# Moving the query product of the HGRN decay levels to GpSimd and one convolution tap back to VectorE, with the exponents of each level computed in its own turn

## The reference

```python
proj = xn @ w_in + b_in
(h_q, h_f_fwd, h_f_bwd, h_i, h_g, m_q, m_k, m_v, m_o, gates...) = split_cols(proj, IN_SPLITS)
q_h = to_heads(silu(h_q));  v_h = to_heads(h_i)
lf  = lower_bounded_log_forget(h_f, lb);  k = -expm1(lf)          # for each direction
# HGRN2: S_t = diag(f_t) S_{t-1} + k_t v_t^T,  o_t = S_t^T q_t,  both directions added
#   score(t, s) = sum_d q[t,d] * k[s,d] * exp(cum[t,d] - cum[s,d])
hgrn_out = head_rmsnorm(o_h) * silu(h_g)
qk  = silu(centred_dwconv(concat(m_q, m_k), conv_w, conv_b))      # 5 taps along the tokens
# mLSTM over qk, m_v and the gates, both directions, then the output projection
```

## Time and profile before

| | us |
|---|---|
| median of 3 runs | 1890.41 |
| the runs | 1887.72, 1890.41 and one of 5112.27 |
| the profiled execution, its own time | 1887.72 |
| its span on the core | 1885.9 |
| TensorE busy | 1780.3 |
| VectorE busy | 964.3 |
| ScalarE busy | 665.6 |
| GpSimd busy | 155.8 |

### The profile page before, as it was taken

One profiled execution on the slowest core, in us unless ns is written; L12 is line 12 of the kernel. 1 busy time (PEld: TensorE's weight loads), 2 busy tenths in 40 slices (PEclk: granted clock), 3 DMA queues, 4 the chain that ended last, 5 costly groups with the idle time before them and its releaser, 6 DMA issues.

```text
span 1885.9 us, 18182 instructions
## 1 busy us (share of the span) xinstructions
PE 1780.3 (94%) x6946; PEld 1246.3 (66%) x6946; DVE 964.3 (51%) x1328; ACT 665.6 (35%) x993; POOL 155.8 (8%) x160
## 2 busy tenths in 40 slices
PE   7999898988899999998999898989998999999997
PEld 1378643355688888886765455446886778888886
DVE  5657555355464424433476676377543254434343
ACT  2531244312343313325442542543543243323132
POOL 0302200014200000003000000023200100000001
PEclk9999999999999999999999999999999999999999
DMA  9324310421213232223131111101521122222331
GB/s 320 113 92 157 112 35 11 152 94 45 91 51 117 79 112 90 89 84 117 45 111 64 70 45 45 48 0 63 184 89 46 45 89 90 89 89 89 113 109 44
DMA packets 98353, 166.26 MB, mean 88 GB/s; under 512 B 3371, under 2 KB 39723, under 8 KB 98092
## 3 DMA queue, kind: packets, MB, share of 16 engines
q1 hardware_dynamic: 94524, 152.63, 23.5%
q0 software_dynamic: 3760, 12.72, 2.1%
HBM read 163.23 MB, written 2.10 MB: 88 GB/s over the span
## 4 chain that ended last, share of the span: by engine, by line
PE 84%; DVE 6%; ACT 5%; issue 2%; DMA 1%; POOL 1%; SPq 0%; DVEq 0%; ACTq 0%; POOLq 0%
PE bank L726 12%; PE bank L727 12%; PE bank L728 12%; PE bank L759 6%; PE bank L760 6%; PE bank L764 5%; PE bank L713 4%; PE bank L939 3%; PE bank L780 3%; PE bank L1107 3%; PE bank L1165 2%; PE bank L969 2%; PE bank L829 1%; PE bank L982 1%; PE bank L909 1%
## 5 line engine op out<-in xcount | busy, mean ns | idle before, releaser
L2650 POOL TENSOR_TENSOR arena<-arena 128x512 f32<-128x512 f32 (+1 forms) x56 | 72.7, 1308 | 985.4 <-ACT arena L1335 981.6
L759 PE MATMUL bank<-xn_hi,weights_hi 128*128 128x512 f32 x320 | 127.4, 398 | 6.2 <-ACT xn_hi L1320 6.2
L760 PE MATMUL bank<-xn_hi,weight_slots_lo 128*128 128x512 f32 x320 | 127.1, 397 | 0.0
L1315 ACT ACTIVATE weights_hi<-weight_slots 128x2048 fp32r<-128x2048 f32 (+2 forms) x46 | 77.0, 1725 | 121.5 <-DMA weight_slots<-in_ffn_w_down 67.1
L1871 ACT ACTIVATE weights_hi<-weight_slots 128x2048 fp32r<-128x2048 f32 x30 | 55.8, 1908 | 162.8 <-DMA weight_slots<-in_w_up 109.1
L713 PE MATMUL bank<-arena,weight_slots 128*128 128x512 f32 x256 | 112.2, 592 | 0.0
L726 PE MATMUL bank<-xn_hi,weights_hi 128*128 128x512 f32 x288 | 112.0, 389 | 0.0
L727 PE MATMUL bank<-xn_lo,weights_hi 128*128 128x512 f32 x288 | 112.0, 389 | 0.0
L728 PE MATMUL bank<-xn_hi,weight_slots_lo 128*128 128x512 f32 x288 | 112.0, 389 | 0.0
L2607 DVE TENSOR_TENSOR weight_slots_lo<-weight_slots,weights_hi 128x2048 fp32r<-128x2048 f32 x30 | 67.4, 2289 | 86.3 <-ACT weights_hi L1871 86.3
L1302 ACT ACTIVATE arena<-bank 128x512 f32<-128x512 f32 (+3 forms) x110 | 54.7, 538 | 139.6 <-PE bank L728 50.6
(11 more groups left out here) (402 smaller groups left out, 3822.8 us busy)
## 6 DMA issues: line engine op xcount, KB each, us to landing
weight_slots<-in_w_in SPq DMA_DIRECT2D x30, 1024.0 KB, 7.2
weight_slots<-in_ffn_w_up SPq DMA_DIRECT2D x22, 1024.0 KB, 7.2
weight_slots<-in_w_mod SPq DMA_DIRECT2D x16, 1024.0 KB, 7.6
weight_slots<-in_w_up SPq DMA_DIRECT2D x16, 1024.0 KB, 6.4
weight_slots<-in_w_down SPq DMA_DIRECT2D x16, 1024.0 KB, 6.4
arena<-in_w_mod POOLq DMA_DIRECT2D x32, 256.0 KB, 3.4
weight_slots<-in_w_out SPq DMA_DIRECT2D x8, 1024.0 KB, 7.4
weight_slots<-in_w_xkv SPq DMA_DIRECT2D x8, 1024.0 KB, 7.5
```

The costliest lines, as they stand in the source:

```text
L759: mm(ps[:, 0:width], wh(k, m), x2[0][:, k, 0:width], start=k == 0, stop=False)
L760: mm(ps[:, 0:width], wl(k, m), x2[0][:, k, 0:width], start=False, stop=False)
L1315: A(high(kind, n)[:, a:b], W[:, s_, a:b], ACT.Copy).then_inc(w_hi, 1)
L2650: G.tensor_tensor(acc, acc, sq[i % 2][:, 0:width], ALU.add).then_inc(sq_added, 1)
```

## The change

There are three edits, which belong together.

1. The product of B with the queries (18 instructions of 128x1024) goes from VectorE to GpSimd. GpSimd's list gets it between the load of the bias rows and the wait for ho_3; a step of level 0, which has no such product, gets a one-element copy that only raises B_ready. TensorE waits for B_ready at every step, level 0 included.
2. The centre tap of the convolution and the semaphore conv_mid go: VectorE computes it as its own first instruction of five, and ScalarE only evicts the product.
3. VectorE's order in a step: the exponents of step n now stand in step n, ahead of the masked copies of the step before and of `keys_decayed` of n, and no longer one step ahead.

```diff
@@ TensorE, level()
                 pe.wait_ge(sem("A_ready"), n + 1)
-                if lev:
-                    pe.wait_ge(sem("B_ready"), n - hp)
+                pe.wait_ge(sem("B_ready"), n + 1)
@@ ScalarE, projection_out()
                     free(A(raw_[:, m, :], ps[:], ACT.Identity, bias=b), f"{kind}_{m}")
-                if kind in ("mq", "mk"):
-
-                    o, c0 = (mq, 0) if kind == "mq" else (mk, HC)
-                    evicted(act, f"{kind}_{m}")
-                    if kind == "mk":
-                        act.wait_ge(sem("conv_done"), HC)
-                    A(o[:, m, :], raw_[:, m, :], ACT.Identity, scale=pc("mlstm_conv_w_2", 16 + c0 + m),
-                      bias=pc("mlstm_conv_b_2", c0 + m)).then_inc(sem("conv_mid"), 1)
@@ VectorE, keys_decayed()
                 V.tensor_tensor(Ar, Ar, split(kb, hp, lev)[1], ALU.mult).then_inc(sem("A_ready"), 1)
-                dve.wait_ge(sem("decay_B"), n - hp)
-                B_ = AB[n % 2][1]
-                V.tensor_tensor(B_, B_, q2[:, 1024 * hp:1024 * hp + 1024], ALU.mult).then_inc(sem("B_ready"), 1)
@@ VectorE, projection_out()
-                    dve.wait_ge(sem("conv_mid"), c0 + m + 1)
+                    link(V.tensor_scalar(o[:, m, :], r_[:, m, :], w[2], pc("mlstm_conv_b_2", c0 + m), ALU.mult, ALU.add))
@@ VectorE, the loop
                         for hp, lev in groups[g]:
-                            i = steps.index((hp, lev))
-                            if i == 0:
-                                exponents(hp, lev)
+                            exponents(hp, lev)
+                            scores_out()
                             keys_decayed(hp, lev)
-                            scores_out()
-                            if i + 1 < len(steps):
-                                exponents(*steps[i + 1])
                             pending.append((hp, lev))
@@ GpSimd, after the load of the bias rows
+            for m in range(HC):
+                evicted(pool, f"hq_{m}")
+            for hp, lev in steps:
+                n = steps.index((hp, lev))
+                q_ = q2[:, 1024 * hp:1024 * hp + 1024]
+                B_ = AB[n % 2][1]
+                if lev == 0:
+                    G.tensor_copy(pool_note[:], eps[:]).then_inc(sem("B_ready"), 1)
+                else:
+                    pool.wait_ge(sem("decay_B"), n - hp)
+                    G.tensor_tensor(B_, B_, q_, ALU.mult).then_inc(sem("B_ready"), 1)
```

More of the change, by code:

```diff
@@ L2714, in _ @@
             load(tiles(82, 2), io["bias_rows"].partition_broadcast(P).rearrange("p (a t) -> p a t", a=2), "bias_rows")
+            steps = hgrn_steps()
+            for m in range(HC):
[9 more added lines that the diff above has]
+                    G.tensor_tensor(B_, B_, q_, ALU.mult).then_inc(sem("B_ready"), 1)
             done(pool, "ho_3")
```

## The result

The changed kernel took 1903.81 us, the median of five runs (1901.11 to 1907.23), against 1887.72 before, the median of five too: two more executions of the kernel before have come to the three in the table above. The ratio is 1.0078, 95% interval 1.0056 to 1.01, or 14.7 us more (10.6 to 19). It is taken over more executions than the medians, eleven of the changed kernel from 1895.12 to 1907.23 us, so it isn't quite the ratio of the two medians, which differ by 16.1 us. The forecast was 1903.0, with 13.4 us more by its sum and 1 more for the clock. The profiled execution took 1901.32.

What follows compares the result with a forecast made beforehand. TensorE, busy for 94% of the span, was the bound, with VectorE's rounds slightly longer (8.98 against 8.66 us) in the mq and mk part. Terms summed to +13.4 us, 1901.1; allowing for the median and 1 us of clock, 1903, range 1892 to 1912.

Steps and rivals of the forecast that it cites:

- GpSimd's product, 2.37 us: Query product of 128x1024 on GpSimd: 2.37 us, from a line between lengths 512 and 2048; bounds 1.29 and 4.52.
- Both engines at once: GpSimd's product and VectorE instructions with two SBUF operands run one after the other, costing VectorE 2.17 us per product.
- Which instruction is blocked: On VectorE, the second half of the keys or an exponent takes 2.7 to 2.9 us instead of 0.68 in most rounds.
- After mq_0: VectorE's eviction, centre tap, taps and the level's chain make the level ready at 1051.6 against 1048.64: +2.9 us.
- After mq_1: VectorE's round is 10.47 us against TensorE's 8.66: +1.8 us.
- Level 512: First pair, level 512 behind level 256: 6.0 us where it was 5.04, a term of +1.0 us.
- Clock: Longer waits of TensorE can also cost clock: 1 us added to the sum.
- Norms: Norms of heads 0 and 1: ScalarE's silu starts after mq_3's eviction without the 0.81 us tap, -0.9 us.
- Behind mk_3: TensorE already waited 2.39 us there for ScalarE's table; VectorE is now late by about as much: -0.2 us.
- No blocking: Rival, 13%: GpSimd's product runs beside VectorE in the stage, so the terms sum to 4.7 us: 1894 us.
- Not slower: Rival, 5%: VectorE's round shrinks from 8.98 to 8.3 us, waits at level 512 and behind mk_3 go: -5, 1883.
- The clock falls as well: Rival, 15%: TensorE's longer waits bring the half clock, three falls of 1.2 to 3.5 us each: +7, 1910 us.

Runs made afterwards that it cites:

- spare kernels: Two kernels: the kernel before, with GpSimd also computing a 128x1024 product nobody needs (ratio 1.0075), or filling tiles with zeros instead (ratio 1.0001).
- the spare writes: The kernel before, with GpSimd also filling two free tiles twice with zeros that nobody needs: 1890.00 against 1890.32 us, ratio 1.0001.
- one level each: The kernel before with each of the 20 decay levels behind a TensorE product of its own, none sharing one: 1872.39 against 1890.32 us, ratio 0.9913.

## Why the prediction was right, point by point

- *GpSimd's product, 2.37 us.* It takes 2.34 undisturbed. The mean of 3.05 in the page is over my 2.4 to 2.8, since the records count the time in which GpSimd stands ready and lets VectorE pass. I had named 3 us and more as a sign of being wrong that would put the mv levels over 8.66; it came, and the mv levels stayed 8.7 us apart.
- *Both engines at once*, the term that decides: right. 2.83 us for 0.68 is 2.15 of blocking where I had 2.17, a key half or an exponent is held like this in 11 of the 18 rounds, and the pair of spare kernels shows it by itself. The product alone cost 8.3 us.
- *Which instruction is blocked*: half right. I named a key half or an exponent. In the rounds behind mq_0 and mk_1 it was the next centre tap, which I had priced by its length alone, and in that behind mk_2 in part (1.01 us). There GpSimd let both key halves pass, so that the level waited for its product and not, as I had it, for the second half behind it. The sum is nearly the same: from the first exponent at 1045.01 to level 128 at 1052.23 are 7.2 us, as forecast.
- *After mq_0*: forecast +2.9, measured 3.7 - 0.6 = +3.1. *After mq_1*: forecast +1.8, measured +4.2, in the second profile +1.7. The step that failed in the first is "by then GpSimd stands ready, its product goes first": it stood ready at 1059.13 and let six instructions go ahead. It cost nothing in the end, because those six included the exponents of level 512.
- *Level 512*: in sum 6.25 forecast, 6.5 and 6.4 measured.
- *Clock.* I gave it 1 us. The slices of the kernel after (length, busy PE, PEld, DVE, ACT, POOL, then the granted clock):

```profile
1060.00:1070.00 10.00, 6.01 (x23) 4.84 (x22) 8.33 (x7) 2.77 (x4) 8.37 (x3) 0.72 0.01 2
1070.00:1080.00 10.00, 10.00 (x30) 5.89 (x29) 3.55 (x5) 3.41 (x7) 0.00 (x0) 0.94 0.00 0
1170.00:1180.00 10.00, 8.41 (x32) 4.55 (x31) 10.00 (x11) 2.80 (x3) 5.39 (x2) 1.00 0.13 49
```

  Behind the wait of 3.99 us TensorE ran at 1.2 GHz for a while, so level 512 took 4.86 us instead of the 3.69 in the earlier trace rows: +1.2. At the last level 512 it was the other way round, 5.38 against 6.10: -0.7. The slice from 1170, at 0.68 before, is at 1.00 now, because VectorE and with it the wait came later. In sum +0.5 here, and some 3 in the second profile: the 1 lies between, with more spread than I gave it. Nor does a wait's length settle it: I had noted that the 3.10 us at 1062 cost no clock, and with the spare writes the same wait did, 1.7 us.
- *Norms* -0.9: with the 1.2 of clock, 6.5 + 1.2 - 0.9 = 6.8, as measured. *After mk_1* +2.9: measured 3.1. *After mk_2* +1.8: 1.8. *Behind mk_3* -0.2: -0.6, a term I had sized 0.4 us too small. *Level 64* +1.8: 1.8. *Last 256* +1.75: 1.7. *Last 512* 0: 0.
- *No blocking* (1894) falls by the spare kernels and the blocked rows. *Not slower* (1883) falls by the result. *The clock falls as well* (1910) is what the second profile of the change went halfway to, 3 us and not 7.
- *Behind the stage nothing gets shorter*: 678.6 and 678.5 us.

So the forecast's sum held at nearly every place because each term was tied to a start in the trace. That the median came within 1 us of it is in part luck: the same kernel took 1906.16 us the second time, its stage 2.7 us longer by the clock alone. By the ratios the three edits cost about 8, 4 and 0 us, and the 4 isn't clear of nothing in the run by itself. The edit that looks most like relief is the dear one: it takes 1.13 us per level off VectorE and in most rounds puts 2.15 us of standing still in its place.

## What to carry to other kernels

Before moving an elementwise instruction to an idle engine, look in the trace for one row in which both engines work at once on two SBUF operands: here one such pair gave the term that decided, and the mean busy time (8% and 51%) pointed the wrong way. A fixed order that hands a level's inputs over one turn ahead was worth some 3 to 5 us over twenty levels here, where both engines' rounds are within 0.3 us of each other. And where TensorE waits only at turns that carry two pieces of work, spread the pieces before you speed up an engine: that gave 9 us in the stage where the speed-up cost 14.

## What was unexpected of the hardware

- A VectorE instruction with a single SBUF tensor input is held as well: TENSOR_SCALAR of 128x512 took 0.55 us alone and 2.36 beside GpSimd's product. The Trainium skill, page "SBUF — State Buffer", section "Who interferes with whom", says this of a `tensor_scalar` that enters a mode with two ports; the trace agrees that it is held. That it ran in such a mode no run shows; its 0.55 us against 0.68 for a product of the same size would fit.
- VectorE instructions that take one operand from PSUM were not held. In the kernel with the product alone on GpSimd six masked copies ran whole inside a product, at 0.72 to 0.74 us, and three of the additions with the bias at 0.69. One pair, GpSimd and VectorE:

```profile
1003.19 2.36 POOL L2723 TENSOR_TENSOR arena<-arena 128x1024 f32<-128x1024 f32 x1 [5.94 <-ACT arena L1646]
```
```profile
1004.33 0.74 DVE L2377 COPY_PREDICATED arena<-level_masks,bank 128x512 f32<-128x512 uint8 x1 [0.20 <-PE bank L1094]
```

- GpSimd doesn't always get in at the next gap. With its record starting 0.00 to 0.02 us behind that of the first key half it waited for one VectorE instruction (2.87 us at 1175.45), for two (3.46 at 1048.66) or for about six (5.9 at 1059.13), the last once in two profiles of the same kernel. What decides this is open.
- The same instructions take different times ahead of the stage. From the start to hi_0 thirteen profiles took from 964.0 us (the order alone) to 973.0 (the tap alone), though no edit touches that part. The largest piece is one group of 64 products, in the first kernel and then in the second:

```profile
L969 PE MATMUL bank<-arena 128*128 128x512 f32 x64 | 29.6, 622 | 1.8 <-ACT arena L1302 1.8
```
```profile
L969 PE MATMUL bank<-arena 128*128 128x512 f32 x64 | 33.4, 687 | 1.8 <-ACT arena L1302 1.8
```

  That is 3.8 us, and the granted clock of the slice from 360 to 480 us was 0.97 in the one and 0.91 in the other. Such differences are as large as the effects studied here, which is why one level each gains 16.4 us by the ratio and 8.9 by the stage: 3.0 us lay ahead of the stage in its profile and 2.2 behind it, and I can't say how much of the rest is the kernel's.
